# First norm and input projection of a hybrid decoder layer joined into one program

## The reference, cut to what matters

```python
def rms_norm(x, g):
    y = xf * lax.rsqrt(jnp.mean(xf * xf, axis=-1, keepdims=True) + RMS_EPS)
    return y * g

h = jnp.concatenate([meta, x], axis=1)      # 16 + 512 rows
hn = rms_norm(h, ln_mix_g)
proj = hn @ w_in                            # 2048 x 5632, all float32
aq, ak, av, hq, hf, hi, hg = split(proj)
```

## Time and profile before

| | us |
|---|---|
| median of three runs | 3456.09 (3454.34 to 3456.39) |
| the profiled execution, its own time | 3455.83 |
| its span, first to last instruction | 3454.0 |
| first projection product begins | 38.21 |
| first matmul of piece 1 | 92.63 |
| first transpose of attention | 572.81 |

### The profile page before, as it was taken

The page is one execution under the profiler, slowest core; times in us unless marked ns, Lnnn a source line. Parts: engine busy times, 40 slices in busy tenths (PEclk is TensorE's granted clock), DMA queues, the critical chain, the costliest instruction groups (busy, mean ns, idle before and its releaser), DMA issues.

```text
span 3454.0 us, 51138 instructions
## 1 busy us (share of the span) xinstructions
PE 3313.4 (96%) x16860; PEld 2918.5 (84%) x16860; DVE 2198.0 (64%) x3868; ACT 1113.2 (32%) x1724; POOL 1162.4 (34%) x872
## 2 busy tenths in 40 slices
PE   7999998999999976999999999999999999999999
PEld 5778876888777865899899899899989989989988
DVE  2003412881158997777777777777777777777776
ACT  3222223552222287222323222323222232322231
POOL 2344432354445500333322232232233333333332
PEclk9999999999999999999999999999999999999999
DMA  4233330004322146888888888788888878878887
GB/s 144 79 87 97 92 91 22 26 19 140 102 93 85 62 170 235 274 298 286 263 270 266 264 271 263 261 274 265 265 264 270 263 264 271 266 264 269 266 261 234
DMA packets 294659, 687.05 MB, mean 199 GB/s; under 512 B 139040, under 2 KB 139296, under 8 KB 292000
## 3 DMA queue, kind: packets, MB, share of 16 engines
q1 hardware_dynamic: 220848, 417.52, 37.3%
q0 software_dynamic: 73728, 268.47, 23.1%
HBM read 655.48 MB, written 30.41 MB: 199 GB/s over the span
## 4 chain that ended last, share of the span: by engine, by line
PE 60%; ACT 2%; issue 1%; ACTq 0%; DMA 0%; DVE 0%; DVEq 0%
PE exp_o L2139 10%; PE exp_o L2137 10%; PE exp_o L2141 10%; PE exp_a L2120 10%; PE exp_a L2118 10%; PE exp_a L2119 10%; ACT table_gaps L1882 2%; ACT table_stage L1898 1%; DMA gate_table<-table_stage 0%; PE table_b L1842 0%; ACTq L1882 0%; ACTq L1898 0%; DMA exp_gates<-gate_table 0%; ACT table_hot L1886 0%; PE table_t L1833 0%
## 5 line engine op out<-in xcount | busy, mean ns | idle before, releaser
L2120 PE MATMUL exp_a<-x_high,exp_ul 128*128 128x384 f32 x1984 | 663.1, 334 | 0.0
L2118 PE MATMUL exp_a<-x_high,exp_uh 128*128 128x384 f32 x1984 | 663.0, 334 | 0.0
L2119 PE MATMUL exp_a<-x_low,exp_uh 128*128 128x384 f32 x1984 | 662.9, 334 | 0.0
L2137 PE MATMUL exp_o<-exp_vh,exp_ah 128*128 128x512 f32 x1536 | 598.8, 390 | 13.4 <-DVE exp_al L2276 13.4
L2139 PE MATMUL exp_o<-exp_vl,exp_ah 128*128 128x512 f32 x1536 | 599.2, 390 | 0.0
L2141 PE MATMUL exp_o<-exp_vh,exp_al 128*128 128x512 f32 x1536 | 599.1, 390 | 0.0
L2099 POOL DMA_INDIRECT exp_rows<-in_v_rows,exp_now x256 | 329.0, 1285 | 708.3 <-DVE h L2230 656.4
L2099 POOL DMA_INDIRECT exp_rows<-in_u_rows,exp_now x256 | 300.5, 1174 | 688.0 <-DVE exp_rows L2223 640.6
L2169 ACT CAST exp_vh<-exp_raw 128x1024 fp32r<-128x1024 f32 x252 | 255.7, 1051 | 504.0 <-PE exp_o L2141 495.1
L2209 DVE TENSOR_TENSOR exp_vl<-exp_raw,exp_vh 128x1024 fp32r<-128x1024 f32 x256 | 304.4, 1220 | 159.6 <-ACT exp_vh L2169 152.5
L2118 PEld LDWEIGHTS exp_a<-x_high,exp_uh 128*128 128x128 f32 x1984 | 372.4, 188 | 1.2
(11 more groups left out here) (319 smaller groups left out, 5189.0 us busy)
## 6 DMA issues: line engine op xcount, KB each, us to landing
exp_raw<-in_v SPq DMA_DIRECT2D x256, 512.0 KB, 4.5
exp_raw<-in_u SPq DMA_DIRECT2D x248, 512.0 KB, 5.2
w_in_raw<-in_w_in SPq DMA_DIRECT2D x88, 512.0 KB, 3.6
gate_table<-table_stage SPq DMA_DIRECT2D x5, 4096.0 KB, 11.6
exp_gates<-gate_table SPq DMA_DIRECT2D x126, 160.0 KB, 7.7
w_out_raw<-in_w_out SPq DMA_DIRECT2D x32, 512.0 KB, 3.7
w_q_raw<-in_w_q SPq DMA_DIRECT2D x32, 512.0 KB, 3.9
x_rows<-in_x SPq DMA_DIRECT2D x4, 1024.0 KB, 8.1
```

The source lines that it names most:

```text
L2118: pe.matmul(bank, uh[:, b, c, :], xh[:, 0:DENSE_TB, c, :], start=(c == 0), stop=False)
L2119: pe.matmul(bank, uh[:, b, c, :], xl[:, 0:DENSE_TB, c, :], start=False, stop=False)
L2120: last = pe.matmul(bank, ul[:, b, c, :], xh[:, 0:DENSE_TB, c, :], start=False, stop=(c == DC - 1))
L2137: pe.matmul(bank[:, :], ah[:, key, tokens], vh[:, dc % 2, key, :], start=(key == 0), stop=False)
```

## The change

The first norm is no longer a program; `norm_rows` is left for the second norm alone. `project` takes the raw rows of x and the meta rows. In it:

- SP issues two copies of the meta rows (to partitions 0 to 15 and 16 to 31), x tiles 0 and 1, weight step 0, x tiles 2 and 3, weight steps 1 to 3, and then the late constants. The attention mask is no longer among these; it is loaded at the start of `attend`.
- PE transposes the meta rows, then columns 0 to 2 of each x tile as it lands. The other 13 columns are transposed in piece 0, column c + 3 behind the products of column c, through a ring of three banks. High and low parts are made from the unscaled rows, with the gain.
- Squares are summed in between: ACT the meta rows and tile 2 ahead of the columns and tile 3 after column 5, DVE tiles 0 and 1. The means follow DVE's column 7, the root ACT's column 9, the inverse roots DVE's column 10.
- Banks of natural pieces are emptied with a multiply by the factor of the row (one number for each partition), the meta rows likewise. For the turned pieces the factor changes along the free axis, so DVE spreads it to a 128 x 512 tile, PE transposes that after piece 0, DVE copies it to `rstd_row` ahead of piece 7's banks, and all four banks of a turned piece are emptied by DVE with a multiply of two tensors.
- POOL does the first two low parts of the weights, then `narrow_mask`, then the rest.

Core of the diff (PE, then DVE, ACT, attention and the loads; the removed body of the first norm, placements and semaphores are left out):

```diff
-            for s in spent:
-                sp.sem_clear(s)
+            load_rows(sp, x_loaded, meta_loaded)
             stream.load_rest(sp, PIECES)
         @block.gpsimd
         def _(pool):
             pool.memset(nat_meta[:, KV_PIECE, KVH * HD:], 0.0).then_inc(meta_cleared, 1)
+            stream.split_first_low(pool)
+            narrow_mask(pool)
             stream.split_low_rest(pool, PIECES)
...
+            def turn_x(tb, c):
+                return pe.transpose(turn_banks[c % TURN_BANKS][:, tb, :], x_rows[:, tb, c * P:(c + 1) * P],
+                                    ident[:, :])
+            def first_columns():
+                pe.wait_ge(early_in, early_count)
+                pe.wait_ge(meta_loaded, 32)
+                for c in range(DC):
+                    last = pe.transpose(meta_turn[:, c, :], meta_rows[0:M, c * P:(c + 1) * P], ident[0:M, 0:M])
+                last.then_inc(meta_x_turned, 1)
+                for tb in range(TB):
+                    pe.wait_ge(x_loaded[tb], 16)
+                    for c in range(TURN_BANKS):
+                        last = turn_x(tb, c)
+                        if tb == TB - 1:
+                            last.then_inc(x_turned, 1)
+            def next_column(c):
+                pe.wait_ge(x_low, c - TURN_BANKS + 1)
+                for tb in range(TB):
+                    last = turn_x(tb, c)
+                last.then_inc(x_turned, 1)
+            def spread_row():
+                pe.wait_ge(x_low, DC)
+                pe.wait_ge(spread_ready, 1)
+                for tb in range(TB):
+                    last = pe.transpose(turn_banks[2][:, tb, :], spread[:, tb, :], ident[:, :])
+                last.then_inc(row_ready, 1)
             def natural(p, with_meta):
+                turning = isinstance(p, int) and p == 0
                 for g in range(STEPS):
                     stream.await_step(pe, p, g)
                     for s in range(SPAN):
                         c = g * SPAN + s
                         w = stream.parts(g, s)
+                        if turning:
+                            pe.wait_ge(x_low, c + 1)
+                        if turning and c == 0:
+                            pe.wait_ge(meta_ready, 1)
                         for tb in range(TB):
...
+                            last = meta_product(p, c, w, p + 1)
+                        if turning and s == 0 and c + TURN_BANKS < DC:
+                            next_column(c + TURN_BANKS)
                     stream.release(last)
+                    if turning and c + TURN_BANKS < DC:
+                        next_column(c + TURN_BANKS)
                     if g == 1 and isinstance(p, int) and p:
                         fold_meta(p - 1)
+            first_columns()
             for p in range(META_PIECES + 1):
                 natural(p, p < META_PIECES)
+                if p == 0:
+                    spread_row()
...
             def empty_natural(p):
                 for tb in (0, 2):
                     dve.wait_ge(unit_done, p * 3 + (tb + 1))
-                    dve.tensor_copy(nat[:, p, tb, :], banks[tb][:, :]).then_inc(even_free, 1)
+                    dve.tensor_scalar(nat[:, p, tb, :], banks[tb][:, :], rstd[:, tb:tb + 1], None, ALU.mult)\
+                        .then_inc(even_free, 1)
             def empty_turned(p):
-                for cb in (0, 2):
-                    dve.wait_ge(unit_done, p * 3 + (cb + 1))
-                    dve.tensor_copy(turned[:, p * 4 + (cb - 4 * NAT_PIECES), M:L], banks[cb][:, :])\
-                        .then_inc(even_free, 1)
+                for cb in range(4):
+                    if cb < 3:
+                        dve.wait_ge(unit_done, p * 3 + (cb + 1))
+                    else:
+                        stream.await_piece(dve, p)
+                    dve.tensor_tensor(turned[:, p * 4 + (cb - 4 * NAT_PIECES), M:L], banks[cb][:, :],
+                                      rstd_row[:, :], ALU.mult).then_inc((even_free, odd_free)[cb % 2], 1)
...
+            def split_meta():
+                dve.wait_ge(meta_x_turned, 1)
+                dve.tensor_tensor(meta_whole[:, :, :], meta_turn,
+                                  x_gain[:, :].unsqueeze(2).to_broadcast([P, DC, M]), ALU.mult)\
+                    .then_inc(meta_whole_ready, 1)
+                dve.wait_ge(meta_high, 1)
+                dve.tensor_tensor(hn[0][:, :, M:2 * M], meta_whole[:, :, :], hn[0][:, :, 0:M].bitcast(F32),
+                                  ALU.subtract).then_inc(meta_ready, 1)
+            def sum_rows(tb):
+                dve.wait_ge(x_loaded[tb], 16)
+                if tb:
+                    dve.wait_ge(summed_too, tb)
+                dve.scalar_tensor_tensor(x_squares[1][:, :], x_rows[:, tb, :], 1.0, x_rows[:, tb, :],
+                                         ALU.mult, ALU.mult,
+                                         accum_out=x_stat[:, 0, tb:tb + 1]).then_inc(summed_too, 1)
+            def mean_rows():
+                dve.wait_ge(summed, 3)
+                dve.wait_ge(summed_too, 2)
+                dve.tensor_scalar(x_stat[:, 1, 0:TB + 1], x_stat[:, 0, 0:TB + 1], 1.0 / D, EPS,
+                                  ALU.mult, ALU.add).then_inc(x_meaned, 1)
+            def spread_rstd():
+                dve.wait_ge(x_rooted, 1)
+                inverse_root(dve, link, *(x_stat[:, k, 0:TB + 1] for k in (3, 1, 2, 0)))
+                dve.sem_inc(normed, 1)
+                dve.tensor_copy(spread[:, :, :], rstd.unsqueeze(2).to_broadcast([P, TB, P]))\
+                    .then_inc(spread_ready, 1)
+            dve.memset(x_stat[:, 0, :], 1.0).then_inc(cleared, 1)
             link(dve.memset(stat[:, :, 0, :], 1.0))
+            dve.wait_ge(early_in, early_count)
+            dve.wait_ge(cleared, 1)
+            split_meta()
+            for tb in range(2):
+                sum_rows(tb)
+            for c in range(DC):
+                dve.wait_ge(x_high, c + 1)
+                dve.scalar_tensor_tensor(x_columns(hn[1], c), turn_banks[c % TURN_BANKS][:, :, :], x_gain[:, c:c + 1],
+                                         x_columns(hn[0], c).bitcast(F32), ALU.mult, ALU.subtract)\
+                    .then_inc(x_low, 1)
+                if c == 7:
+                    mean_rows()
+                elif c == 10:
+                    spread_rstd()
             with dve.Fori(0, HG_PIECE) as p:
...
+            dve.wait_ge(row_ready, 1)
+            link(dve.tensor_copy(rstd_row[:, :], turn_banks[2][:, :, :].rearrange("p b t -> p (b t)")))
             for p in range(NAT_PIECES, GATE_PIECE):
```

```diff
-                    act.copy(nat[:, p, tb, :], banks[tb][:, :]).then_inc(odd_free, 1)
+                    act.activation(nat[:, p, tb, :], banks[tb][:, :], ACT.Copy,
+                                   scale=rstd[:, tb:tb + 1]).then_inc(odd_free, 1)
                 if with_meta:
                     if p:
                         act.wait_ge(meta_folded, p)
-                    act.copy(meta_row[:, :], meta_bank[0:2 * M, :]).then_inc(meta_stacked, 1)
+                    act.activation(meta_row[:, :], meta_bank[0:2 * M, :], ACT.Copy, scale=meta_rstd)\
...
+            def stack_turned(p):
+                stream.await_piece(act, p)
+                act.activation(meta_row[:, :], meta_bank[0:2 * M, :], ACT.Copy, scale=meta_rstd)\
...
-            splits(0, range(2, STEPS))
+            def sum_squares(rows, m, at, count):
+                if count:
+                    act.wait_ge(summed, count)
+                act.activation(x_squares[0][0:m, :], rows, ACT.Square,
+                               accum_out=x_stat[0:m, 0, at:at + 1]).then_inc(summed, 1)
+            act.wait_ge(cleared, 1)
+            act.wait_ge(meta_loaded, 32)
+            sum_squares(meta_rows[:, :], 2 * M, TB, 0)
+            act.wait_ge(meta_whole_ready, 1)
+            act.copy(hn[0][:, :, 0:M], meta_whole[:, :, :]).then_inc(meta_high, 1)
+            stream.split_ahead(act, 0)
+            act.wait_ge(x_loaded[2], 16)
+            sum_squares(x_rows[:, 2, :], P, 2, 1)
+            for c in range(DC):
+                act.wait_ge(x_turned, c + 1)
+                act.activation(x_columns(hn[0], c), turn_banks[c % TURN_BANKS][:, :, :], ACT.Copy,
+                               scale=x_gain[:, c:c + 1]).then_inc(x_high, 1)
+                if c == 1:
+                    stream.split_ahead(act, 1)
+                elif c >= 4 and c % SPAN == 0:
+                    splits(0, [c // SPAN])
+                if c == 5:
+                    act.wait_ge(x_loaded[3], 16)
+                    sum_squares(x_rows[:, 3, :], P, 3, 2)
+                elif c == 9:
+                    act.wait_ge(x_meaned, 1)
+                    act.activation(x_stat[:, 2, 0:TB + 1], x_stat[:, 1, 0:TB + 1], ACT.Sqrt).then_inc(x_rooted, 1)
             splits(1, [0])
+            act.wait_ge(normed, 1)
             empty_natural(0, True)
...
-            act.wait_ge(gated, 8)
```

(15 more changed lines are left out.)

## The result

| | before | after |
|---|---|---|
| median (lowest to highest of 5 runs each), us | 3454.34 (3450.26 to 3456.39) | 3435.77 (3435.10 to 3437.39) |
| ratio, 95% interval | | 0.995 (0.9938 to 0.9961) |
| span of the profiled execution | 3454.0 | 3434.0 |
| first product | 38.21 | 18.86 |
| first matmul of piece 1 | 92.63 | 78.81 |

The change gains 18.6; 10.6 were forecast, and the range ended 4 us too high. The profile says where the rest is: 14.1 us are gained when attention starts, and 20.0 at the end. 7.7 of the profiled execution's gain arise in the routing, whose instructions the change doesn't touch (a spell of the slow clock in the output projection gives 2 back before it).

A forecast was written before the change was run, and what follows sets the result against it. PE, busy for 96% of the span, was taken as the bound, standing still at the start. Terms -19.6 + 9.5 - 0.5, the rest 0, gave -10.6 us: 3456.09 to 3445.5, range 3440.0 to 3452.0.

The forecast's parts named there:

- (1): Start of PE: last x tile lands at 16.3, first product at 18.6 instead of 38.21, saving 19.6 us.
- The cover: Start: the first weight step's low part on POOL is done at 15, 3.5 us ahead of need; PE pays any excess.
- (2): Piece 0: 14 insertions of four transposes at 0.65 each (0.44 plus 0.21 break), 9.1, plus 0.4 for slow clock: 9.5 us lost.
- Rival A: Cheap insertions at 0.44 each, break hidden, last tile on time: 13.5 us saved, 3442.6; chance 0.16.
- (3): Piece 0: PE does not wait for columns, since each is transposed three columns ahead of its use; cost 0.
- C: Piece 0: PE falls into step with the column chain, 26 us more, 3471.5; chance 0.03.
- (4): Start of products: the slow clock costs as much as before, 0 within 2.6 us either way.
- D: The clock stays low through piece 0, +55 us less 10.6, 3500.5; chance 0.03.
- (5) to (7): Bank evacuations cost 0; the projection's end gains 0.5 us; the mask load in attention costs 0 with 3.7 us cover.
- Afterwards nothing depends on absolute time, so the gain is kept to the end: Stages behind the changed part: the 10.6 us gain carries unchanged to the end.

The follow-up runs named there:

- turn_first: The changed kernel with all 16 columns transposed and split before the first product, none between products: 3444.41 us, ratio 0.9975.
- warm: The changed kernel with 24 more transposes of the identity where PE waits for x tiles 2 and 3 and for the first split: 3433.99 us, ratio 0.9942.
- before_later: The kernel before with 40 more products ahead of piece 0, so that everything behind starts later: 3464.76 us, ratio 1.0034.
- late18: The changed kernel with 8 more products on PE behind step 2 of routing head 2, making PE 1.8 us late: 3436.88 us, ratio 0.9953.
- before_dve3: The kernel before with 3 tiny clears more on VectorE alone, in the first microseconds: 3448.96 us, ratio 0.9989.

## Why the prediction was wrong

(1) *First product*: 18.86 for 18.6. Right, by its own chain: last tile 16.77 for 16.3, and from there 2.1 for 2.3. The cover was thinner than forecast, 2.2 for 3.5: GpSimd's split took 3.62 and ended at 16.53, not at 15.

(2) *Transposes between products*: the mis-sized term. 0.45 for 0.65, over 14 insertions 2.8 us, and 0.4 more that I had set aside for insertions at the slow clock; the first one, at 24.24, stands behind the rise. I had added the 0.21 of break read from small matmuls of 32 rows. Against a stream of products four transposes showed the pitch of 0.11 and nothing else. Rival A had this price, and its 13.5 is near the 14.1 of the touched part.

(3) *Waits in piece 0*: none, as forecast. C did not happen; turn_first shows what lies that way: 8 us.

(4) *Cold clock*: the slow spell is 0.9 shorter, worth 0.5. Inside the bound. D did not happen. By the Trainium skill (TensorE: Matmul & The Clock Gate, Part 4: PE-mode transpose) a transpose does not count as busy for the clock in the way a product does. The trace disagrees: behind warm's 24 transposes the products stand 0.23 apart from 19.22 on, without them 0.43 until 23.26.

(5) to (7) *Evacuations, end of projection, mask*: no wait on the banks, -0.4 for -0.5 (last product to attention 3.68 before, 3.31 after), the mask in time with 3.6 to spare for 3.7.

*"Afterwards nothing depends on absolute time, so the gain is kept to the end"*: the step that failed most. Of time it is true (before_later, late18, turn_first and warm shift the routing by -2 to +10 and it keeps its course). But I took from it that untouched stages cost the same, and they don't: the sum had 0 for them, the medians have 4.5 (18.6 - 14.1) and the profiles 5.9 (7.7 in the routing, less 2 in the output projection). The routing hangs, among other things, on where VectorE's instructions stand in their list: before_dve3 moves that alone, and both long waits (4.4) are gone.

The terms up to attention add up: 10.6 forecast + 3.3 (-0.3 + 2.8 + 0.4 + 0.5 - 0.1) is 13.9 of 14.1. With them alone right, the forecast would have been 3442, still above the measured time. That before_dve3's 4.3 and the missing 4.5 are alike proves little, with an interval from 0.7 to 6.9.

A rival to the long wait is the clock, and it has a share. Of 99 executions of the old kernel the 35 with a mean granted clock of 0.987 average 3455.7, the 26 at 0.989 3450.9, the 11 at 0.990 3449.0; the changed kernel has 3436.2 at 0.989 and 3434.3 at 0.990. At one and the same clock the two are 14.7 apart, little more than the touched part's 14.1. The two go together in the profiles: near 7 of the 8 waits of 3.51 a spell of granted clock 0.50 begins, within 1.3 us of the wait's end, and near none of the waits of about 1.3. So part of what the long waits cost may come as slow clock behind them; how much, and why the spell behind head 2's wait of 1.9 is there in some kernels and not in after, no run parts. The lowest executions of all, before 3447.97 and after 3434.17, are 13.8 apart; no profile caught such a run of the old kernel.

The lock is what I could have known. By the Trainium skill (SBUF — State Buffer, Who interferes with whom) issue order decides which of VectorE and GpSimd is blocked, for the whole instruction; the rows above agree: 0.03 ahead 0.23, 0.14 behind 2.34. Head 6's long wait, in before and before_later and in no other, is the same lock: there the tie of head 5 was lost by 0.008 and 0.009, elsewhere it stood between 0.10 ahead and 0.001 behind. What moves it by hundredths, and what delays VectorE by 0.12 to 0.17 in head 2, stays open.

## What to carry to other kernels

Price transposes between products by their pitch (0.11 each here) and don't add a break that was read from small matmuls. Look in the untouched stages for a tie between VectorE and GpSimd on work with two SBUF operands: if a small instruction starts within some 0.2 us of a long one on the other engine, any edit elsewhere can move the time by several us, and a few padding instructions on one engine are a cheap test. Before crediting a change with its whole gain, compare stage by stage, and ask of each stage it didn't touch why it moved; look at the granted clock beside the waits.

## What the hardware showed that I had not expected

- A delay of 0.12 to 0.17 on VectorE that moved by one instruction when one was taken out in front, vanished with three more, and turned into 2.25 on PE through a tie for the lock. The same tie was lost a second time, by 0.008, without it.
- Transposes of the identity bring PE to 2.4 GHz for the products behind them (0.23 apart from 19.22 on, against 0.43 until 23.26), while the profile's row of granted clock says 1.00 in both, as the stretches show, after and then warm:

```profile
19.00:23.00 4.00, 4.00 (x10) 3.13 (x11) 1.17 (x2) 1.07 (x2) 2.37 (x1) 1.00 0.68 215
```

```profile
19.00:23.00 4.00, 4.00 (x20) 3.11 (x21) 1.22 (x2) 1.24 (x3) 2.41 (x1) 1.00 0.72 238
```

- GpSimd's first split took 3.62 in place of 2.37 when VectorE squared a tile beside it: the same rivalry the other way.
